# Router logits of a two-layer mixer and mixture network: from 32 short products to 8 long ones in column groups, with a summing product behind them

## What is computed

```python
# each of the two layers of the second block
h = h + concatenate([r_out, h_out], -1) @ w_out     # (256, 1024) @ (1024, 1024)
xn = rms_norm(h, norm2_g)
affinity = softmax(xn @ w_router, axis=-1)          # (256, 1024) @ (1024, 16)
gate, idx = top_k(affinity.T, 32)                   # 32 tokens for each expert
xe = xn[idx]
hid = silu(xe @ w_gate) * (xe @ w_up)               # 16 experts, 1024 x 1024 each
ye = hid @ w_down * gate
h = h + scatter_add(ye, idx)
```

## Time and profile before

| | us |
|---|---|
| median of 3 runs | 1898.38 |
| lowest, highest | 1897.21, 1900.1 |
| the profiled execution | 1899.93 |
| its span in the trace | 1898.1 |
| TensorE matmul busy | 1495.6 (79%) |
| VectorE busy | 789.5 (42%) |
| ScalarE busy | 576.9 (30%) |
| GpSimd busy | 62.7 (3%) |
| moved from memory | 558.16 MB, 295 GB/s over the span |

### The profile page before, as it was taken

The page is one execution under the profiler, slowest core; times in us unless marked ns, Lnnn a source line. Parts: engine busy times, 40 slices in busy tenths (PEclk is TensorE's granted clock), DMA queues, the critical chain, the costliest instruction groups (busy, mean ns, idle before and its releaser), DMA issues.

```text
span 1898.1 us, 26290 instructions
## 1 busy us (share of the span) xinstructions
PE 1495.6 (79%) x11260; PEld 1125.8 (59%) x11260; DVE 789.5 (42%) x1237; ACT 576.9 (30%) x906; POOL 62.7 (3%) x56
## 2 busy tenths in 40 slices
PE   8999999999999999996635546379999654545546
PEld 8999999899999899982201212039998221111212
DVE  4557777556777788750100101018964010010101
ACT  4455545445555576330000000017533000000001
POOL 1010000101000000100000000002010000000000
PEclk9999999999999999999877868689999886786868
DMA  9317555431755394599999999998468999999997
GB/s 300 125 34 244 192 186 186 131 112 37 269 178 189 101 284 148 178 363 419 430 430 430 429 429 429 431 407 268 134 219 352 431 430 429 430 431 429 430 430 317
DMA packets 174186, 560.90 MB, mean 296 GB/s; under 512 B 12209, under 2 KB 134503, under 8 KB 146295
## 3 DMA queue, kind: packets, MB, share of 16 engines
q1 hardware_dynamic: 165558, 551.49, 74.5%
q10 hardware_dynamic: 8512, 7.74, 1.3%
HBM read 558.16 MB, written 1.05 MB: 295 GB/s over the span
## 4 chain that ended last, share of the span: by engine, by line
PE 56%; issue 22%; DMA 16%; DVE 4%; ACT 1%; POOL 0%; SPq 0%; POOLq 0%; ACTq 0%; DVEq 0%; PEldq 0%
PE psum L2583 8%; PE psum L2553 5%; PE psum L2844 5%; PE psum L2530 5%; DMA ring<-in_w_down 4%; PE psum L2532 4%; PE psum L2531 4%; DMA ring<-in_w_up 3%; DMA arena<-in_w_gate 3%; PE psum L2699 2%; PE psum L2826 2%; PE psum L2448 2%; PE psum L2650 2%; DMA arena<-in_w_up 2%; DMA arena<-in_w_down 2%
## 5 line engine op out<-in xcount | busy, mean ns | idle before, releaser
L2844 PE MATMUL psum<-ring,arena 128*32 128x512 f32 (+1 forms) x1600 | 281.8, 694 | 199.2 <-DMA ring<-in_w_down 78.7
L2844 PE MATMUL psum<-arena 128*32 128x512 f32 x1024 | 206.9, 699 | 148.6 <-DMA ring<-in_w_up 40.9
L2844 PEld LDWEIGHTS psum<-ring,arena 128*32 128x32 f32 x1600 | 71.0, 128 | 347.2 <-issue 344.7
L917 DVE TENSOR_TENSOR W<-ring,W 128x2048 fp32r<-128x2048 f32 (+1 forms) x96 | 213.9, 2228 | 123.2 <-ACT W L912 122.9
L912 ACT ACTIVATE W<-ring 128x2048 fp32r<-128x2048 f32 (+1 forms) x96 | 178.4, 1860 | 84.1 <-PE psum L2532 40.0
L2530 PE MATMUL psum<-XT,W 128*128 128x256 f32 x704 | 200.1, 284 | 0.2
L2173 DVE TENSOR_TENSOR arena<-arena,psum 128x512 f32<-128x512 f32 x16 | 11.0, 690 | 454.1 <-PE psum L2844 454.1
L2532 PE MATMUL psum<-XT,W 128*128 128x256 f32 x704 | 199.2, 283 | 0.0
L2531 PE MATMUL psum<-XT,W 128*128 128x256 f32 x704 | 199.1, 283 | 0.0
L2844 PEld LDWEIGHTS psum<-arena 128*32 128x32 f32 x1024 | 50.5, 126 | 250.2 <-issue 250.2
L2583 PE MATMUL psum<-rounded_slot,rounded_slot 128*128 128x256 f32 x1216 | 177.1, 285 | 0.7 <-DVE rounded_slot L817 0.7
(11 more groups left out here) (331 smaller groups left out, 2626.0 us busy)
## 6 DMA issues: line engine op xcount, KB each, us to landing
ring<-in_w_down SPq DMA_DIRECT2D x36, 2048.0 KB, 29.7
ring<-in_w_up SPq DMA_DIRECT2D x32, 2048.0 KB, 31.1
ring<-in_w_up SPq DMA_DIRECT2D x58, 1024.0 KB, 5.2
ring<-in_w_in SPq DMA_DIRECT2D x56, 1024.0 KB, 7.0
ring<-in_w_gate SPq DMA_DIRECT2D x28, 2048.0 KB, 33.6
arena<-in_w_up SPq DMA_DIRECT2D x24, 2048.0 KB, 33.0
arena<-in_w_down SPq DMA_DIRECT2D x20, 2048.0 KB, 29.8
arena<-in_w_gate SPq DMA_DIRECT2D x20, 2048.0 KB, 29.9
```

Of the source, the lines that this page charges most:

```text
L917: nc.vector.tensor_tensor(W2[split_pair(v)][:, c], slot(v % SLOTS_1)[:, c], W1[split_pair(v)][:, c].bitcast(F32), ALU.subtract).then_inc(r ...
L2844: last = nc.tensor.matmul(psum[CAP * e:CAP * (e + 1), b, 0:cols.stop - cols.start], src[:, 4 * half + k, CAP * e:CAP * (e + 1)], tiles[e][ ...
```

## The change

The router's operands trade places. `raw_logits(i)` now holds 32 weight columns stationary (16 of the router, 16 zeros that GpSimd writes) and moves 256 tokens past them, one product for each k, into the 32 partitions of group k % 4 of bank 4. The four partial sums are copied out by VectorE and summed and turned back by a product with a 0/1 selection table into bank 6. The first turned half is rounded in two pieces of 256 columns with a wait of its own for k=5. The last two retention products come behind the first transpositions, and ScalarE rounds half b=3 ahead of its last four squares. The table and the wider weights add 144 columns to the arena.

```diff
+WIDE = 32
+    put("partial_sum", np.arange(P)[:, None] % WIDE == np.arange(EXPERTS)[None, :])
@@ memory
-        wr = place(KD * EXPERTS).rearrange("p (k n) -> p k n", k=KD)
+        wr_wide = place(KD * WIDE).rearrange("p (k n) -> p k n", k=KD)
+        wr = wr_wide[:, :, 0:EXPERTS]
+        partial_logits = place(S)
@@ GpSimd
                 pool.wait_ge(small2, past(small2) + 48)
+                pool.memset(wr_wide[:, :, EXPERTS:WIDE], 0.0)
@@ ScalarE
                 for t in range(TT):
+                    if t:
+                        turn_mixer_act(act, past, 1, 3)
                     act.wait_ge(r_mixed, past(r_mixed) + t + 1)
...
-                turn_mixer_act(act, past, 1, 3)
                 round_out(4)
...
-                    last = nc.scalar.activation(elog[:, t], psum[:, 4, ...], ACT.Exp, ...)
+                    last = nc.scalar.activation(elog[:, t], psum[:, 6, ...], ACT.Exp, ...)
@@ VectorE
-                turn_mixer_dve(dve, past, 0, 2)
-                turn_mixer_rest(dve, 0, 2, xt_dve, past(xt_dve) + 3)
+                dve.wait_ge(turned, past(turned) + 6)
+                for k in (4, 5):
+                    src = psum[:, 0, (k - 4) * S:(k - 3) * S]
+                    nc.vector.tensor_copy(mixed_first[:, k, :], src).then_inc(xt_dve, 1)
+                    dve.wait_ge(xt_dve, past(xt_dve) + k - 1)
+                    nc.vector.tensor_tensor(mixed_rest[:, k, :], src, mixed_first[:, k, :].bitcast(F32), ALU.subtract).then_inc(xt_rest, 1)
                 dve.wait_ge(mix_sq, past(mix_sq) + TT * HEADS + TT)
                 nc.vector.tensor_scalar(rsm[:, 0:TT * HEADS], ssm[:, 0:TT * HEADS], 1.0 / HD, EPS, ALU.mult, ALU.add).then_inc(mix_arg, 1)
                 turn_mixer_rest(dve, 1, 3, xt_act, past(xt_act) + 3)
...
+                dve.wait_ge(logits, past(logits) + 1)
+                nc.vector.tensor_copy(partial_logits, psum[:, 4, 0:S]).then_inc(xt_dve, 1)
                 dve.wait_ge(rms, past(rms) + 2)
                 nc.vector.tensor_scalar(linv, rs, -1.0, None, ALU.mult).then_inc(scaled, 1)
-                dve.wait_ge(logits, past(logits) + 1)
-                lg = psum[:, 4, 0:TT * EXPERTS].rearrange("p (t e) -> p t e", t=TT)
+                dve.wait_ge(logits, past(logits) + 2)
+                lg = psum[:, 6, 0:TT * EXPERTS].rearrange("p (t e) -> p t e", t=TT)
@@ TensorE
-                            if i == t == 0 and k % 2 == 0:
-                                pe.wait_ge(xt_rest, past(xt_rest) + 1 + {4: 1, 6: 2, 0: 3, 2: 4}[k])
+                            if i == t == 0 and (k % 2 == 0 or k == 5):
+                                pe.wait_ge(xt_rest, past(xt_rest) + 1 + {4: 1, 5: 2, 6: 3, 0: 4, 2: 5}[k])
...
                 def raw_logits(i):
-                    for t in range(TT):
-                        for k in (2 * i, 2 * i + 1):
-                            last = nc.tensor.matmul(psum[:, 4, t * EXPERTS:(t + 1) * EXPERTS], raw_turned[:, k, t * P:(t + 1) * P], wr[:, k, :],
-                                                    start=(t == k == 0), stop=(k == KD - 1), skip_group_check=True)
+                    for k in (2 * i, 2 * i + 1):
+                        at = WIDE * (k % 4)
+                        last = nc.tensor.matmul(psum[at:at + WIDE, 4, 0:S], wr_wide[:, k, :], raw_turned[:, k, :],
+                                                start=(k < 4), stop=(k >= 4), skip_group_check=True)
...
-                pe.wait_ge(mix_done, past(mix_done) + TT)
-                for nth, b in ((0, 2), (1, 3)):
-                    turn_half(nth, b)
+                for t in range(TT):
+                    for h in range(HEADS):
+                        if (t, h) == (TT - 1, HEADS - 1):
+                            pe.wait_ge(mix_done, past(mix_done) + TT)
+                            for nth, b in ((0, 2), (1, 3)):
+                                turn_half(nth, b)
+                        for i in range(TT):
+                            last = nc.tensor.matmul(psum[:, 2 + t, h * HD:(h + 1) * HD], RS[:, h, i, t * P:(t + 1) * P],
+                                                    rv[:, i, h * HD:(h + 1) * HD], start=(i == 0), stop=(i == 1))
+                    last.then_inc(r_mixed, 1)
...
                 raw_logits(3).then_inc(logits, 1)
+                pe.wait_ge(xt_dve, past(xt_dve) + 10)
+                for t in range(TT):
+                    last = nc.tensor.matmul(psum[:, 6, t * EXPERTS:(t + 1) * EXPERTS], partial_logits[:, t * P:(t + 1) * P],
+                                            table("partial_sum"), start=True, stop=True)
+                last.then_inc(logits, 1)
                 idle_products(3, IDLE_PRODUCTS["softmax"])
```

More of the change, by code:

```diff
@@ L39 @@
 SLOT_W = 8 * 256
-ARENA = 22312
+ARENA = 22456
 USES_1 = 48
@@ L281 @@
     "up_products_scaled": (22, 0, 0), "turned_in_psum": (13, 13, 0), "turned_first_parts_by_dve": (4, 0, 0), "turned_first_parts_by_act": (12, 1, 0),
-    "turned_second_parts": (19, 5, 0), "weights_first_parts": (49, 24, 0), "weights_second_parts": (49, 24, 0),
-    "hidden_before_the_split": (12, 0, 0), "hidden_first_parts": (12, 0, 0), "turned_by_dve": (2, 8, 0),
+    "turned_second_parts": (19, 6, 0), "weights_first_parts": (49, 24, 0), "weights_second_parts": (49, 24, 0),
+    "hidden_before_the_split": (12, 0, 0), "hidden_first_parts": (12, 0, 0), "turned_by_dve": (2, 10, 0),
     "turned_by_act": (2, 4, 0), "projected": (16, 0, 0), "bank_emptied_by_act": (6, 0, 0),
@@ L1519, in _ @@
                 for t in range(TT):
-                    last = nc.scalar.activation(elog[:, t], psum[:, 4, t * EXPERTS:(t + 1) * EXPERTS], ACT.Exp, scale=linv[:, t:t + 1],
+                    last = nc.scalar.activation(elog[:, t], psum[:, 6, t * EXPERTS:(t + 1) * EXPERTS], ACT.Exp, scale=linv[:, t:t + 1],
                                                 bias=lmax[:, t:t + 1], accum_out=lsum[:, t:t + 1])
@@ L2098, in _ @@
                 turn_mixer_dve(dve, past, 2, 0)
-                turn_mixer_rest(dve, 2, 0, xt_dve, past(xt_dve) + 4)
+                turn_mixer_rest(dve, 2, 0, xt_dve, past(xt_dve) + 5)
                 turn_mixer_rest(dve, 3, 1, xt_act, past(xt_act) + 4)
@@ L2712, in raw_logits @@
                 def raw_logits(i):
-                    pe.wait_ge(xt_dve, past(xt_dve) + 4 + i + 1)
+                    pe.wait_ge(xt_dve, past(xt_dve) + 5 + i + 1)
                     if i == 0:
                         pe.wait_ge(gated, past(gated) + 1)
-                    for t in range(TT):
-                        for k in (2 * i, 2 * i + 1):
-                            last = nc.tensor.matmul(psum[:, 4, t * EXPERTS:(t + 1) * EXPERTS], raw_turned[:, k, t * P:(t + 1) * P], wr[:, k, :],
-                                                    start=(t == k == 0), stop=(k == KD - 1), skip_group_check=True)
-                    return last
-                pe.wait_ge(mix_done, past(mix_done) + TT)
-                for nth, b in ((0, 2), (1, 3)):
-                    turn_half(nth, b)
+                    for k in (2 * i, 2 * i + 1):
+                        at = WIDE * (k % 4)
+                        last = nc.tensor.matmul(psum[at:at + WIDE, 4, 0:S], wr_wide[:, k, :], raw_turned[:, k, :],
+                                                start=(k < 4), stop=(k >= 4), skip_group_check=True)
+                    return last
+                for t in range(TT):
[8 more added lines that the diff above has]
+                    last.then_inc(r_mixed, 1)
                 for i in range(4):
```

2 lines of the change are left out of this document (1 added, 1 removed).

## The result

The change made the kernel slower: 1906.11 us median (1905.11 to 1908.90, 5 runs) against 1898.38 (1897.21 to 1900.27, 5 runs), a ratio of 1.0039 with a 95% interval of 1.0028 to 1.0050. That is 7.7 us. I had forecast 1900.3 and given the range up to 1903.5. The profiled execution took 1908.90 (span 1907.0), 2.8 over its median; it lost 2.06 against the profiled execution of before in the first 16 us of its span, far ahead of the change. Two later executions of other kernels lose 2.2 at the same place (f4_before_512, h1_ring_64), the other fourteen between -0.3 and 0.7.

What follows compares the result with a forecast made beforehand. It took the expert weight stream as the bound, its restart set by the mixer-router chain. Added 0.57 + 0.41 = 0.98 us a layer, 1.96 for two, gave 1898.38 + 1.96 = 1900.3 us; range 1896.2 to 1903.5.

Steps and rivals of the forecast that it cites:

- What bounds the kernel: Expert stages: full DMA stream sets the pace; the mixer-router chain moves its restart microsecond for microsecond, gains up to 3 us.
- Part one: Output projection: first product 0.7 us earlier, but k=6 waits for ScalarE's squares, so TensorE ends 0.57 later a layer.
- Part two: Router logits: VectorE gets them 0.41 us later a layer, `raw_logits` savings counted; +0.1 to +0.6 by selection price.
- The burst of two column groups: Each `raw_logits`: groups run side by side, 0.65 us in place of 0.80, saving 0.15.
- my estimate from the Trainium skill: `raw_logits`: at the skill's 79% of ideal, 0.43 would be 0.54, the whole sum 0.7 us more; not adopted.
- the copy and the selection: New router work before VectorE gets the logits: copy of 128x256 0.42 us, selection 0.74 with hand-overs.
- At no cost: ... the wider layout moves addresses: Memory layout: the wider layout only moves addresses, priced at no cost, as were the filling and table.
- Rival 2, the clock: Router to gathers: changed idle times spare both layers the lower clock, 1.2 us each back, 1897.9; chance 0.17.
- Rival 4, the slow clock over the first expert products: First expert products: lower clock still holds, their 3.64 us grow by up to 3.6 a layer, 1904 to 1907; chance 0.06.
- Rival 3, groups one after the other: `raw_logits`: two groups not side by side, three bursts 0.43 us more each, 1.3 a layer, 1902.9; chance 0.12.

Runs made afterwards that it cites:

- f4_before_512: Kernel before with 96 unused columns (384 bytes a partition) ahead of the expert slots; 1905.19 us, ratio 1.0026.
- h1_ring_64: Kernel before with 16 unused columns ahead of the ring and 48 ahead of the expert slots, slots still on a 256-byte multiple; 1900.67 us, ratio 1.0006.
- e2_part_one: Kernel before with only the change's halves, moved retention products and ScalarE order, old logits and layout; 1900.00 us, ratio 1.0001.
- e3_logits: Changed kernel with the old order of retention products and rounding restored, new logits and layout kept; 1904.63 us, ratio 1.0029.
- e1_layout: Kernel before with only the change's memory layout, including table and zero filling, none of its other new work; 1903.88 us, ratio 1.0027.
- g6_after_256: Whole changed kernel with pair_gain moved to the arena's end, so expert slots start at 573 x 256 bytes; 1900.62 us, ratio 1.0007.
- e0_again: Changed kernel run once more, unaltered; 1905.95 us against 1899.12 for the kernel before, ratio 1.0035.
- f2_before_64: Kernel before with only 16 unused columns (64 bytes a partition) ahead of the expert slots; 1904.09 us, ratio 1.0025.
- g7_ring_256: Kernel before with 32 unused columns ahead of the ring and 32 ahead of the expert slots, both on 256-byte multiples; 1898.61 us, ratio 0.9995.
- f1_layout_128: Kernel before with the change's memory layout and 16 unused columns ahead of the expert slots; 1904.92 us, ratio 1.0027.
- g5_layout_256: Kernel before with the change's memory layout, pair_gain moved to the arena's end so expert slots start at 573 x 256 bytes; 1899.81 us, ratio 1.0003.
- h2_behind_slots: Kernel before with 16 unused columns right behind the expert slots, slots unmoved; 1898.81 us, ratio 1.0001.
- h3_best: Kernel before with ring, slots, last home on 256-byte multiples, plus halves, moved products, VectorE's half-1 and half-3 rests before its squares wait; 1898.26 us, ratio 0.9995.

## Why the prediction was wrong, point by point

- **What bounds the kernel: half right.** The restart of the stream moved with the chain, 1.03 for 1.01. But I used the full slices as proof that the stream behind it keeps its length. A DMA share of 9 says that the engines are occupied. It says nothing on how much they move, and the GB/s line does.
- **Part one, 0.57 a layer: right** in sign, place and releaser, 0.5 in the trace, 0.60 and 0.67 in that of e2_part_one. Its time, ratio 1.0001, neither shows twice that nor rules it out.
- **Part two, 0.41 a layer: right within 0.12** (0.45 and 0.53 in e3_logits). The burst of two column groups takes the 0.65 that the earlier trace rows gave. By my estimate from the Trainium skill ("TensorE: Matmul & The Clock Gate", section "Measured speedup vs the span model") it would have been 0.11 more; the trace keeps the row's price. The three bursts ahead of the copy, the copy and the selection came out within 0.1 of their prices.
- **The step that failed is "At no cost: ... the wider layout moves addresses".** It was worth 4.8 us (e1_layout), more than all the rest, and it got one clause that set it to nothing and named nothing that would cover it. Nothing could: the moved addresses are targets of the one resource that I had just called the bound. In its place the runs showed slower rows in both expert stages, 427.9 GB/s in place of 429.9.
- **Rival 2, the clock: real, of about the size I gave it, and no explanation of the result.** From the logits to the issue that ends the hole takes 14.4 where the lower level falls into it, as before in both layers, and 13.0 where it does not, so 1.4 for my 1.2. g6_after_256 and e0_again are spared it in both (granted clock 1.00 over 840 to 860 and 1450 to 1475 in e0_again), and e0_again, the changed kernel itself, still takes 1905.95. Part of what it gains so it loses in the mixer of layer 1, 1.48 at a clock of 0.94 over 1318 to 1345. Whether that mixer has the lower level differs among the slow kernels (in after, e0_again and e1_layout it has, in f2_before_64 and f4_before_512 not) and among the fast ones (in g7_ring_256 it has, in g8_all_256 not).
- **Rival 4, the slow clock over the first expert products: seen, small.** After shows 4.37 in layer 0 where a burst at full clock takes 3.64, but before had 3.87 there itself (849.67 to 853.54), so that is 0.5. The measured 1906.11 lies in this rival's 1904 to 1907 by luck: its cause is not the one at work.
- **Rival 3, groups one after the other: did not happen.**
- **The range was too narrow on the slow side** because it was built of the terms that I had priced. None of them reached past 1903.5 but rival 4.

One thing that the places do stays open. From the gating to the logits f1_layout_128, f4_before_512, g7_ring_256 and g8_all_256 take 33.3, though their engines do the work of the kernel before (32.95 and 32.87). It lies in the projection, whose operands these layouts move as well: on the chain of g7_ring_256 its 48 products take 5.99 and the next 96 take 11.51, before 5.87 and 11.31. Why, no run shows. These 0.4 us a layer are in the kernel with the best time too.

Shown is that the slots' start decides (f2_before_64 in, g5_layout_256 out, h2_behind_slots for what lies behind them), and that it acts on the time of each row of the weight transfers. Argued is why. The Trainium skill has a rule near it ("DMA: Bandwidth & Descriptors", section "How a descriptor splits into AXI transactions"): a transaction has to start at a multiple of 256 bytes, so a descriptor that starts off one begins at the multiple below, and the bytes fetched in vain cost time. The rule is told of bytes that are fetched; here the side that moved is the one written. Estimated by that page, a row of 16384 bytes would be 65 transactions and not 64, 1.6% more. The trace agrees in that the start counts modulo 256 and that a quarter and a half of it cost alike. It does not agree in size: 614.6 for 611.0 ns is 0.6%, the addition is about the same for rows of 2048 bytes, and the first three transfers of a run are spared.

## What to carry to other kernels

When a kernel is bound by a stream of loads, the start address of every load target is a term of the sum. A constant, a wider tile or a pad placed ahead of a buffer moves everything behind it: work out the absolute byte offsets of the load targets before and after, and keep them on multiples of 256 bytes, by moving a small tensor to the end if need be. In the profile compare GB/s in saturated slices, not the DMA share.

## What was not expected of the hardware

Sixty-four bytes cost 4.7 us of 1899 (f2_before_64). A quarter and a half of 256 bytes cost about the same, so it is a step and not a slope. And the cost of loads off the multiple depends on their neighbours: where six of them alternated with four on it, about three in ten paid. The version to keep is g8_all_256, the kernel before with ring, slots and last home on multiples of 256: 1897.33, ratio 0.9990 [0.9981, 0.9998]. It beats both kernels, over the kernel before by little; g7_ring_256 and h3_best, whose weight rows are as fast, measure 0.9995. Of the change itself no part has shown a gain.
